# Unrounded key and value weights on the hardware queue, query weights in halves of rows, and a margin in the order of TensorE's products

## The reference, cut to what matters

```python
h = rmsnorm(x, g_mix_norm)
proj = h @ w_in + b_in                       # [q 512 | k 128 | v 128 | glu_in 1024 | gates 2048]
y_attn = sliding_window_attention(q, k, v, sinks) @ w_attn_proj      # window 128, softmax with a sink per head
y_conv = conformer_conv(glu_in) @ w_conv_proj + b_conv_proj          # a*sigmoid(b), depthwise conv 31, LayerNorm, silu
x = x + (sigmoid(g0) * y_attn + sigmoid(g1) * y_conv) @ w_out
gate, up = split(rmsnorm(x, g_ffn_norm) @ w_ffn_in)
x = x + (silu(gate) * up) @ w_ffn_down
out = rmsnorm(x, g_final)
```

## Time and profile before

| | |
|---|---|
| median of 3 runs | 890.77 us (890.59 to 892.04) |
| profiled execution | 891.32 us, span of its slowest core (core 1) 889.8 us |
| spans of the cores | 882.5 to 889.8 us |
| PE busy on core 1 | 852.6 us, 96% of the span |
| DVE, ACT, POOL busy | 46%, 31%, 25% |
| chain that ended last | PE 88%, DMA 4%, DVE 2%, issue 2%, ACT 2%, POOL 2% |

### The profile page before, as it was taken

The page is one execution under the profiler, slowest core; times in us unless marked ns, Lnnn a source line. Parts: engine busy times, 40 slices in busy tenths (PEclk is TensorE's granted clock), DMA queues, the critical chain, the costliest instruction groups (busy, mean ns, idle before and its releaser), DMA issues.

```text
span 889.8 us, 14080 instructions; the slowest of 8 cores (882.5 to 889.8 us)
## 1 busy us (share of the span) xinstructions
PE 852.6 (96%) x4779; PEld 395.1 (44%) x4779; DVE 411.7 (46%) x613; ACT 275.5 (31%) x434; POOL 226.2 (25%) x271
## 2 busy tenths in 40 slices
PE   3899999899999999999999999999999999999995
PEld 2454444434444444444444444444444444444442
DVE  4554666859734433576321551226321145212287
ACT  3366367556322222244311001110111100111286
POOL 5573176546232222222211001110011000000043
PEclk9899999999999999999999999999999999999999
DMA  9959839359559933651865206531453400000044
GB/s 171 169 127 234 142 80 104 98 120 96 55 49 136 248 36 36 140 110 37 124 66 48 24 10 85 49 36 13 71 49 32 40 1 0 1 1 1 1 179 201
DMA packets 118806, 71.56 MB, mean 80 GB/s; under 512 B 89731, under 2 KB 109361, under 8 KB 118737
## 3 DMA queue, kind: packets, MB, share of 16 engines
q0 software_dynamic: 83088, 29.37, 31.2%
q1 hardware_dynamic: 35232, 41.13, 17.1%
q10 hardware_dynamic: 417, 0.16, 0.1%
HBM read 85.56 MB, written 10.52 MB: 108 GB/s over the span
## 4 chain that ended last, share of the span: by engine, by line
PE 88%; DMA 4%; DVE 2%; issue 2%; ACT 2%; POOL 2%; DVEq 0%; SPq 0%; POOLq 0%; ACTq 0%
PE ps L520 84%; PE ps L875 3%; DMA arena<-w_in 2%; ACT arena L524 2%; DVE arena L546 1%; DMA arena<-x 1%; POOL arena L534 1%; PE ps L839 1%; POOL arena L513 0%; DMA z_scratch<-arena 0%; PE ps L715 0%; DMA arena<-z_scratch 0%; DVE arena L534 0%; DVE arena L540 0%; POOL arena L540 0%
## 5 line engine op out<-in xcount | busy, mean ns | idle before, releaser
L520 PE MATMUL ps<-arena 128*128 128x512 bf16 (+3 forms) x4002 | 807.7, 365 | 15.1 <-DMA arena<-g_mix_norm 4.5
L520 PEld LDWEIGHTS ps<-arena 128*128 128x128 bf16 (+1 forms) x4002 | 367.6, 99 | 445.6 <-issue 35.1
L534 DVE TENSOR_TENSOR arena<-arena,ps 128x512 f32<-128x512 f32 (+1 forms) x216 | 148.4, 687 | 289.9 <-PE ps L520 288.6
L524 ACT ACTIVATE arena<-ps 128x512 f32<-128x512 f32 (+3 forms) x156 | 108.3, 705 | 391.8 <-PE ps L520 371.9
L534 POOL TENSOR_TENSOR arena<-arena 128x512 f32<-128x512 f32 (+3 forms) x85 | 88.8, 1049 | 192.2 <-ACT arena L524 185.3
L524 ACT ACTIVATE arena<-ps,arena 128x512 f32<-128x512 f32 (+1 forms) x112 | 75.3, 687 | 135.4 <-PE ps L520 110.3
L524 ACT ACTIVATE arena<-arena 128x1024 bf16<-128x1024 f32 (+3 forms) x107 | 80.4, 767 | 73.3 <-DVE arena L546 29.7
L546 DVE SCALAR_TENSOR_TENSOR arena<-ps,arena 128x512 f32<-128x512 f32 (+1 forms) x84 | 60.1, 722 | 78.1 <-PE ps L520 76.5
L513 POOL DMA_DIRECT2D arena<-w_ffn_in x44 | 38.8, 883 | 196.5 <-PE ps L520 196.5
L546 DVE SCALAR_TENSOR_TENSOR arena<-arena 128x1024 bf16<-128x1024 f32 (+2 forms) x63 | 66.8, 1063 | 25.0 <-POOL arena L534 20.2
L534 DVE TENSOR_TENSOR arena<-arena 128x512 bf16<-128x512 f32 (+3 forms) x65 | 47.3, 738 | 12.6 <-ACT arena L524 6.4
(11 more groups left out here) (37 smaller groups left out, 102.6 us busy)
## 6 DMA issues: line engine op xcount, KB each, us to landing
arena<-x SPq DMA_DIRECT2D x32, 512.0 KB, 8.4
arena<-w_ffn_in POOLq DMA_DIRECT2D x44, 256.0 KB, 5.4
arena<-z_scratch SPq DMA_DIRECT2D x64, 135.0 KB, 3.2
out<-arena SPq DMA_DIRECT2D x15, 512.0 KB, 2.7
arena<-w_in POOLq DMA_DIRECT2D x16, 256.0 KB, 7.3
arena<-w_in POOLq DMA_DIRECT2D x7, 512.0 KB, 15.6
arena<-w_ffn_down POOLq DMA_DIRECT2D x2, 1536.0 KB, 13.1
arena<-w_ffn_down POOLq DMA_DIRECT2D x2, 1280.0 KB, 20.2
```

What stands on the lines that cost most here:

```text
L520: return S.add("pe", lambda e: e.matmul(out=out, lhsT=lhsT, rhs=rhs, start=start, stop=stop, **kw), r, w, cost=max(0.06, nfree(rhs) * 0.00 ...
L524: return S.add("act", lambda e: e.activation(out=out, in_=in_, func=func, **kw), r, w, cost=0.22 + 0.00089 * nfree(in_))
L534: return S.add(eng, lambda e: e.tensor_tensor(out=out, in0=in0, in1=in1, op=alu), r, w, cost=ecost(eng, nfree(out)))
```

## The change

- Key and value weights: `wkv` is no longer rounded by GpSimd's queue. SyncE loads it as float32 (`wkv_raw`, 1 MB) between x tiles 1 and 2, and GpSimd casts it in two halves.
- Query weights: two transfers of 512 rows by 512 columns instead of 1024 rows by 256 columns. `q_first` accumulates the first half of the rows for all four products, then the second half. `wq_place` puts half of its four copies on ScalarE.
- Gated-unit weights: two transfers of 512 columns instead of four of 256; they wait for x tiles 4 and 7.
- The first four tiles take their 1/rms by ScalarE's Sqrt and VectorE's reciprocal instead of two operations on GpSimd; the first activation of the program becomes Sqrt instead of Exp.
- The transpose of the constants stands behind `hT.3`, the cast of `conv_w` behind `kT.0`.
- The planner: a margin of 0.8 us on whatever a product waits for on another engine, separate streams for GpSimd's and the other queues, small transfers landing after 4 us, and no bank for a product as long as products ahead of it aren't placed.

```diff
-DMA_RATE = 310e3
-SMALL = 0
+DMA_RATE = 290e3
+POOL_DMA_LAT = 3.5
+PE_MARGIN = 0.8
+SMALL = 66000
...
+                if before[i]:
+                    before[i] = {d for d in before[i] if d.end is None}
+                    if before[i]:
+                        return None, None
...
                     if d.eng == "pe" and op.eng == "pe":
                         lat = 0.0
+                    elif op.eng == "pe":
+                        lat += PE_MARGIN
...
                     if op.nbytes <= SMALL:
-                        op.end = t + DMA_LAT
+                        op.end = t + 2 * DMA_LAT
                     else:
-                        dma_free = max(t, dma_free) + op.nbytes / DMA_RATE
-                        op.end = dma_free + DMA_LAT
+                        q = "pool" if e == "pool" else "hw"
+                        s = t + (POOL_DMA_LAT if q == "pool" else 0.0)
+                        dma_free[q] = max(s, dma_free[q]) + op.nbytes / DMA_RATE
+                        op.end = dma_free[q] + DMA_LAT
...
     def cp_(eng, out, in_, r, w):
+        if eng == "act":
+            return act(out, in_, AF.Copy, r, w)
...
-    for tt in range(4):
-        load_x(tt)
+    wkv_raw = A.f32(ZS, 8 * 256).rearrange("p (k m) -> p k m", k=8)
+    load_x(0)
+    load_x(1)
+    dma("sp", wkv_raw, w_in_d[:, K_OFF:K_OFF + 256].rearrange("(k p) m -> p k m", p=128), w=["wkv_raw"])
+    load_x(2)
+    load_x(3)
     dma("act", grow, g_mix_d, w=["grow"])
+    op("pool", lambda e: e.memset(epsb, EPS), w=["epsb"])
+    act(rstd[:, 0:1], epsb, AF.Sqrt, r=["epsb"], w=["rstd0"])
...
-    act(rstd[:, 0:1], epsb, AF.Exp, r=["epsb"], w=["rstd0"])
...
-    wcols(wkv, K_OFF, 256, "wkv", r=["xs0"])
     for hh in range(2):
-        wcols(wq_raw[hh], Q_OFF + 256 * hh, 256, "wq_raw%d" % hh, r=["xs0"])
+        dma("pool", wq_raw[hh], w_in_d[512 * hh:512 * (hh + 1), Q_OFF:Q_OFF + 512].rearrange("(k p) m -> p k m", p=128),
+            r=["xs%d" % hh], w=["wq_raw%d" % hh])
+
+    for hh in range(2):
+        cp_("pool", wkv[:, 4 * hh:4 * hh + 4, :], wkv_raw[:, 4 * hh:4 * hh + 4, :], r=["wkv_raw"], w=["wkv%d" % hh])
...
+    def q_first():
+
+        banks = [next_bank() for _ in range(4)]
+        for kh in range(2):
+            for c in range(4):
+                S.begin()
+                for k in range(4 * kh, 4 * kh + 4):
+                    mm(ps[banks[c].banks[0]], wq[:, k, c, :, :].rearrange("p g d -> p (g d)"), hT[:, k, 0:512],
+                       k == 0, k == 7, r=["wq0.%d" % kh, "wq1.%d" % kh] + hres(0), w=[banks[c]])
+                S.end()
+        for c in range(4):
+            ts_("dve", qT[:, c, :], ps[banks[c].banks[0]], col(c), None, ALU.add, None,
+                r=[banks[c], "cst"], w=["qT.%d" % c])
...
         rms_sq(xst[:, tt, :], tt, 0, "xs%d" % tt)
-        rms_rstd(tt, 1)
+        act(rstd[:, tt:tt + 1], ss[:, tt:tt + 1], AF.Sqrt, r=["ss%d" % tt, "epsb"], w=["rstd%d" % tt], bias=epsb)
+        op("dve", lambda e, tt=tt: e.reciprocal(out=rstd[:, tt:tt + 1], in_=rstd[:, tt:tt + 1]),
+           r=["rstd%d" % tt], w=["rstd%d" % tt])
...
-            for i in range(2):
-                wcols(wglu[2 * i], GLU_OFF + CC + 256 * i, 256, "wglu%d" % (2 * i), r=["xs1"])
-                wcols(wglu[2 * i + 1], GLU_OFF + 256 * i, 256, "wglu%d" % (2 * i + 1), r=["xs1"])
+            wcols(wglu[0], GLU_OFF + CC, 512, "wglu0", r=["xm4"])
+            wcols(wglu[1], GLU_OFF, 512, "wglu1", r=["xm7"])
+            bank_use[0] = ANY
+            q_first()
+            bank_use[0] = ONE
+            return
```

More of the change, by code:

```diff
@@ L176, in schedule @@
                 tiles_of.setdefault(op, []).append(i)
+        before = []
+        for us in self.users:
+            mine = set(us)
+            seen = set()
+            front = set()
+            todo_ = [d for op in us for d in op.order]
+            while todo_:
+                d = todo_.pop()
+                if d in seen or d in mine:
+                    continue
+                seen.add(d)
+                if d.eng == "pe":
+                    if d.block != us[0].block:
+                        front.add(d)
+                else:
+                    todo_.extend(d.order)
+            before.append(front)
         owner = [None] * 8
@@ L225, in schedule @@
         free = {e: 0.0 for e in ENGS}
-        dma_free = 0.0
+        dma_free = {"pool": 0.0, "hw": 0.0}
         left = len(keys)
@@ L438, in record @@
     wq = A.bf16(WAB, 8 * 512).rearrange("p (k h g d) -> p k h g d", k=8, h=4, g=2)
-    wq_raw = [A.bf16(PT + 4096 * g, 8 * 256).rearrange("p (k m) -> p k m", k=8) for g in range(2)]
+    wq_raw = [A.bf16(PT + 4096 * g, 4 * 512).rearrange("p (k m) -> p k m", k=4) for g in range(2)]
     grow = arena_t[0:1, LNR // 4 + 256:LNR // 4 + 1280]
@@ L442, in record @@
     wkv = A.bf16(WAB + 8192, 8 * 256).rearrange("p (k m) -> p k m", k=8)
-    wglu = [A.bf16(WAB + 12288 + 4096 * i, 8 * 256).rearrange("p (k m) -> p k m", k=8) for i in range(4)]
+    wglu = [A.bf16(WAB + 12288 + 8192 * i, 8 * 512).rearrange("p (k m) -> p k m", k=8) for i in range(2)]
     NRING = 14
@@ L650, in record @@
         cp_("dve", gbc[:, 512 * hh:512 * (hh + 1)], ps[bank.banks[0]], r=[bank], w=["gbc.%d" % hh])
-    wcols(wkv, K_OFF, 256, "wkv", r=["xs0"])
     for hh in range(2):
-        wcols(wq_raw[hh], Q_OFF + 256 * hh, 256, "wq_raw%d" % hh, r=["xs0"])
+        dma("pool", wq_raw[hh], w_in_d[512 * hh:512 * (hh + 1), Q_OFF:Q_OFF + 512].rearrange("(k p) m -> p k m", p=128),
+            r=["xs%d" % hh], w=["wq_raw%d" % hh])
+    for hh in range(2):
+        cp_("pool", wkv[:, 4 * hh:4 * hh + 4, :], wkv_raw[:, 4 * hh:4 * hh + 4, :], r=["wkv_raw"], w=["wkv%d" % hh])
+    S.alias(["zs%d.%d" % (c_, j_) for c_ in range(2) for j_ in range(4)], ["wkv_raw"])
     def consts_cols():
@@ L658, in consts_cols @@
         op("pe", lambda e: e.transpose(out=ps[bank.banks[0]][:, 0:NROW], in_=brow, identity=identf[0:NROW, 0:NROW]),
-           r=["brow%d" % i for i in range(7)] + ["identf"], w=[bank], cost=0.3)
+           r=["brow%d" % i for i in range(7)] + ["identf", "hT.3", "hTb.3"], w=[bank], cost=0.3)
         cp_("dve", cst, ps[bank.banks[0]][:, 0:NROW], r=[bank], w=["cst"])
@@ L893, in ln_stats @@
         S.begin()
+        bq = next_bank()
         mm(ps[bm.banks[0]], ones_bf, ysq[:, 0, :], True, True, r=["ones", "ysq.0"], w=[bm])
-        S.end()
-        bq = next_bank()
-        S.begin()
         mm(ps[bq.banks[0]], ones_bf, ysq[:, 1, :], True, True, r=["ones", "ysq.1"], w=[bq])
@@ L931, in wq_place @@
         for h in range(2):
-            cp_("pool" if g and h else "dve", wq[:, :, 2 * h:2 * h + 2, g, :],
-                wq_raw[g].rearrange("p k (h d) -> p k h d", h=4)[:, :, 2 * h:2 * h + 2, :],
+            cp_("act" if h else "dve", wq[:, 4 * g:4 * g + 4, :, h, :],
+                wq_raw[g][:, :, 256 * h:256 * (h + 1)].rearrange("p k (c d) -> p k c d", c=4),
                 r=["wq_raw%d" % g], w=["wq%d.%d" % (h, g)])
@@ L995, in record @@
                     ["wq%d.%d" % (h_, g_) for h_ in range(2) for g_ in range(2)])
-            S.alias(["ring%d.%d" % (i, h) for i in (4, 5) for h in range(2)], ["wkv"])
+            S.alias(["ring%d.%d" % (i, h) for i in (4, 5) for h in range(2)], ["wkv0", "wkv1"])
             w_issue_upto(6)
@@ L1012, in record @@
                 ln_silu(prev, u)
-    S.alias(["ring%d.%d" % (i, h) for i in range(6, 10) for h in range(2)], ["wglu0", "wglu1"])
-    S.alias(["ring%d.%d" % (i, h) for i in range(9, 14) for h in range(2)], ["wglu2", "wglu3"])
+    S.alias(["ring%d.%d" % (i, h) for i in range(6, 10) for h in range(2)], ["wglu0"])
+    S.alias(["ring%d.%d" % (i, h) for i in range(10, 14) for h in range(2)], ["wglu1"])
     w_issue_upto(NRING, after=["zs3.%d" % j_ for j_ in range(4)])
```

17 lines of the change are left out of this document (8 added, 9 removed).

## The result

The changed kernel took 911.1 us (median; 908.0 to 912.1) beside 891.4 us for the kernel before on the same chip: a ratio of 1.0221, 95% interval 1.0201 to 1.0241. The forecast was 893.8 us with a range of 884.5 to 899.5. The profiled execution took 908.03 us, the fastest of the four; its slowest core is core 3, span 906.5 us.

A forecast was written before the change was run, and what follows sets the result against it. TensorE, busy 852.6 of 889.8 us, bounds the kernel, so only its idle time can be won. 891.3 + 8.4 (start) + 1.3 (tables) - 6.7 (middle) = 894.3 us profiled, 893.8 us median; range 884.5 to 899.5 us.

The forecast's parts named there:

- Weights on two queues: At the start, GpSimd's queue is done some 6 us earlier; taken alone, queries end 0 to 2.6 us earlier.
- The added wait: At the start, ScalarE's early exponential waits for the sinks, landing at 21.5 us; queries end at 44.0, not 35.6: +8.4 us.
- The step that failed: Method for the whole kernel: count only when the query products end, then the stalls between 90 and 202 us.
- The tables: A third ScalarE table load, before the first exponential of the scores, adds +1.3 us, or nothing if transposes cover it.
- The middle: Between 90 and 202 us, the margin cuts PE's waits and half clock: -6.7 us, between 0 and -11.
- The second rival: The margin wins nothing in the middle: 899.5 us at most, 896.5 with half of the middle; chance 0.17.
- The third rival: First gated-unit weights land late and hold up PE among score products; makes 884 into some 888 us; chance 0.06.

The follow-up runs named there:

- e6: Changed kernel with the planner of before and ScalarE's exponential of the sinks moved behind tile 4's copy; ratio 1.0025 to the kernel before.
- e1: Changed kernel, recorded order kept, but ScalarE's exponential of the sinks moved behind the copy of the fourth tile's transposes; 902.2 us, ratio 1.0141 to the kernel before.
- e9: Changed kernel, exponential of the sinks behind tile 4's copy, planner's old picture of transfers, margin and bank rule kept; 893.4 us, ratio 1.0019 to the kernel before.
- e2: Kernel before, order kept, but the exponential of the sinks moved ahead of the squarings of tiles 2 and 3; ratio 1.0008 to the kernel before.
- e8: Changed kernel, order kept, but the load of the sinks issued second of ScalarE's eleven small transfers instead of last; 901.7 us, ratio 1.0109 to the kernel before.
- e13: Kernel before with only a planner margin of 0.4 us added; ratio 1.0022 to the kernel before.
- e14: Kernel before with only a planner margin of 1.6 us added; ratio 1.0048 to the kernel before.
- e10: Changed kernel, exponential of the sinks behind tile 4's copy, new planner, first group's gated-unit products behind the second group's keys; 901.3 us, ratio 1.0103 to the kernel before.

## Why the prediction was wrong, by its own steps

**Weights on two queues.** Right in kind: the 3.4 us for w_in are gone, and e6, which holds all of it, shows the queries ending without a wait for weights. It wins nothing in time: they end at 34.99 us in e6 and 36.17 in e1, for 35.62 before.

**The added wait.** Right in place and mechanism: ScalarE idle 11.53 us, released by the sinks at 20.6 us (forecast 21.5), table loads behind it, tile 3's transposes at 29.01. Over-sized: 41.22 us for 44.0, +5.6 for +8.4: the sinks landed 0.9 us earlier, and from the last transposes to the end of the queries it took 12.2 us, not 13.9.

**The step that failed** is "I count the change by when the query products end, and then by the stalls of the middle". Between the two lie 9.6 us. With it fell "in this forecast PE is still behind the fourth tile while they run", by which transfers and order in the first attention block cost nothing. What the runs show in its place is mainly the order that the new picture of transfers writes there: work whose transfer lands late stands early. With the start repaired that block still costs 7 us more than before (e1); with the old picture it costs 2 us more (e9). In the change itself the late scaling of tiles 2 and 3 comes on top. It frees their slots late, so three x tiles are issued from 27.5 us beside a wide gated-unit transfer and take 10 us; ScalarE, GpSimd and PE then wait for them in turn, and the granted clock falls to 0.74 and 0.90 in the two stretches. How the two share the 9.6 us stays open, since no run has the late scaling with the new loads and the old picture. e2 shows that the milestone was wrong in the other direction as well: 2.9 us late there cost nothing.

**The tables.** +1.3 us was mis-sized: e8 keeps them and is no slower than e1, so nothing that can be measured. The page of the Trainium skill (ScalarE: Activation LUTs, Table sets: the hidden batching unit), by which they would have cost 4 us more, is not borne out: 20.63 + 1.28 is followed by the exponential at 21.93, and in e8 11.75 + 1.28 by 13.04, with no room for a drain.

**The middle.** -6.7 us is the other failed term: the stretches show +1.4, and the means of eight cores no change. The two gated-unit products did move, but the wait went to other places: 3.3 us for L574 on core 3, and as means of eight cores 1.5 us won from 90 to 205 us (8.1 for 9.6) and 1.6 lost from 205 to 230 us (1.8 for 0.2). The second rival, that the margin wins nothing, had it (chance 0.17); e13 and e14 show that a margin isn't a gain that scales. One price in the term was wrong from the start, if by little: 0.55 us for the clock counts 5 us at 0.89 where PE was busy for 2.46, which makes 0.27.

**The third rival** was right as a mechanism: with the start repaired (e1) PE waits 4.1 us for the first gated-unit weights. It is one of a family: work that stands early in the order and whose transfer lands late.

**The range** ended at 899.5 us because every upper case took the start's loss to stop at the queries. That the +8.4 and the missing middle gain would both hold gave at most 900; the block between them had no term.

## What to carry to other kernels

A late input is counted to the next place where the chain has room, not to a milestone that is easy to read: follow which slots come free late, which transfers start by them, and what stands first in the order and waits for them. In a planned in-order program the picture of transfers matters as much as costs: when it lets loads land too early, work that needs them stands ahead of other work on every engine, and repairing one engine (e10) moves the wait to another. A planner's constant is tried at three values before its gain is believed.

## What the runs showed of the hardware

The same 4 KB transfer of the sinks took 15.1 us as the last of eleven on ScalarE's queue and 7.6 us as the second, though its queue issued it only 3.8 us earlier: eleven small transfers are not free by being small. A table load beside waits for x cost nothing that 1.0109 against 1.0141 could show. And the half clock was granted for longer than the long waits lasted: in the changed kernel PE was granted 1.2 GHz through most of 44 to 66 us, with waits of 4.0 and 2.0 us at its start and none over 1 us behind them. The stretches there, core 3:

```profile
44.00:55.00 11.00, 7.37 (x36) 3.51 (x36) 6.52 (x11) 6.06 (x9) 1.25 (x2) 0.53 0.74 198
55.00:66.00 11.00, 8.27 (x111) 3.83 (x110) 6.61 (x11) 7.70 (x12) 5.62 (x6) 0.69 0.18 46
```
